# Latent attention: four rows of products a step, and every fourth division moved to VectorE

## What is computed

```
score  = sum over 8 index heads of wi * relu(qi . ki), causal      # choose 128 keys of a query
logits = q_lat . c_sel + bias[distance]                            # 16 heads, chosen keys only
p      = softmax(logits)
o_lat  = p . c_sel
o      = o_lat through w_uv per head;  out = o @ w_o
```

## Time and profile before

| what | value |
|---|---|
| median of three runs | 1882.61 us (1882.45 to 1882.95) |
| the profiled execution | 1882.13 us |
| its span on the core | 1880.9 us |
| PE busy | 1864.3 us, 99% of the span |
| DVE busy | 977.3 us, 52% |
| ACT busy | 674.5 us, 36% |
| POOL busy | 380.7 us, 20% |
| granted PE clock, mean | 0.999 |

### The profile page before, as it was taken

The page is one execution under the profiler, slowest core; times in us unless marked ns, Lnnn a source line. Parts: engine busy times, 40 slices in busy tenths (PEclk is TensorE's granted clock), DMA queues, the critical chain, the costliest instruction groups (busy, mean ns, idle before and its releaser), DMA issues.

```text
span 1880.9 us, 21858 instructions
## 1 busy us (share of the span) xinstructions
PE 1864.3 (99%) x8900; PEld 1503.8 (80%) x8900; DVE 977.3 (52%) x1318; ACT 674.5 (36%) x912; POOL 380.7 (20%) x339
## 2 busy tenths in 40 slices
PE   9999999999999999999999999999999999999998
PEld 8888888888877568888888879778787878888887
DVE  7885543343459864543433447666446454443432
ACT  6743222222234762321212334555323332322213
POOL 2004210010336783210101131111001311110103
PEclk9999999999999999999999999999999999999999
DMA  4322323323333103233232222222232322223221
GB/s 159 112 90 90 112 90 102 100 90 100 97 96 106 53 2 112 90 99 103 90 105 97 76 91 90 68 68 68 84 113 83 108 87 96 90 97 105 90 95 62
DMA packets 167171, 172.36 MB, mean 92 GB/s; under 512 B 7480, under 2 KB 164288, under 8 KB 167072
## 3 DMA queue, kind: packets, MB, share of 16 engines
q1 hardware_dynamic: 164576, 163.76, 27.1%
q0 software_dynamic: 2496, 7.21, 1.2%
HBM read 168.69 MB, written 2.14 MB: 91 GB/s over the span
## 4 chain that ended last, share of the span: by engine, by line
PE 89%; DVE 6%; ACT 3%; issue 2%; DMA 0%; POOL 0%; SPq 0%; DVEq 0%; ACTq 0%
PE bank L775 27%; PE bank L777 27%; PE bank L776 27%; DVE wlo L1699 1%; PE bank L800 1%; DVE XC L1801 1%; PE bank L994 1%; PE bank L1096 1%; PE bank L1113 1%; PE bank L973 1%; ACT whi L1217 1%; ACT pt L1437 1%; PE bank L922 0%; PE bank L1108 0%; PE bank L1162 0%
## 5 line engine op out<-in xcount | busy, mean ns | idle before, releaser
L775 PE MATMUL bank<-Ahi,whi 128*128 128x512 f32 (+2 forms) x1416 | 552.9, 390 | 2.5 <-DVE wlo L1699 0.9
L776 PE MATMUL bank<-Alo,whi 128*128 128x512 f32 (+2 forms) x1416 | 547.8, 387 | 0.0
L777 PE MATMUL bank<-Ahi,wlo 128*128 128x512 f32 (+2 forms) x1416 | 547.7, 387 | 0.0
L1699 DVE TENSOR_TENSOR wlo<-stage,whi 128x2048 fp32r<-128x2048 f32 (+2 forms) x146 | 333.1, 2281 | 381.5 <-ACT whi L1217 381.4
L1217 ACT ACTIVATE whi<-stage 128x2048 fp32r<-128x2048 f32 (+2 forms) x152 | 287.2, 1889 | 443.3 <-PE bank L777 443.3
L775 PEld LDWEIGHTS bank<-Ahi,whi 128*128 128x128 f32 (+1 forms) x1416 | 265.3, 187 | 65.6 <-issue 8.2
L777 PEld LDWEIGHTS bank<-Ahi,wlo 128*128 128x128 f32 (+1 forms) x1416 | 265.3, 187 | 55.1
L776 PEld LDWEIGHTS bank<-Alo,whi 128*128 128x128 f32 (+1 forms) x1416 | 265.4, 187 | 54.8 <-issue 1.2
L775 PE MATMUL bank<-Hhi,whi 128*128 128x512 f32 x688 | 267.7, 389 | 0.0
L777 PE MATMUL bank<-Hhi,wlo 128*128 128x512 f32 x688 | 267.6, 389 | 0.0
L776 PE MATMUL bank<-Hlo,whi 128*128 128x512 f32 x688 | 267.6, 389 | 0.0
(11 more groups left out here) (349 smaller groups left out, 2151.7 us busy)
## 6 DMA issues: line engine op xcount, KB each, us to landing
stage<-in_mlp_w_up SPq DMA_DIRECT2D x32, 1024.0 KB, 5.4
stage<-in_mlp_w_down SPq DMA_DIRECT2D x32, 1024.0 KB, 5.0
stage<-in_w_in SPq DMA_DIRECT2D x22, 1024.0 KB, 4.9
stage<-in_w_ffn_in SPq DMA_DIRECT2D x22, 1024.0 KB, 4.9
stage<-in_w_ffn_out SPq DMA_DIRECT2D x8, 1024.0 KB, 5.1
stage<-in_rec_w_in SPq DMA_DIRECT2D x7, 1024.0 KB, 5.1
stage<-in_att_w_in SPq DMA_DIRECT2D x6, 1024.0 KB, 5.4
stage<-in_rec_w_out SPq DMA_DIRECT2D x4, 1024.0 KB, 4.7
```

Source lines behind the costliest of these rows:

```text
L775: e.matmul(ps, hi, rh, start=first, stop=False)
L776: e.matmul(ps, hi, rl, start=False, stop=False)
L777: return e.matmul(ps, lo, rh, start=False, stop=last)
L1699: e.tensor_tensor(lo_of(u)[:, 0:nk, 0:n], stage[s][:, 0:nk, 0:n], f32(hi_of(u)[:, 0:nk, 0:n]), ALU.subtract).then_inc(s_lo[s], 1)
```

## The change

One step now takes four tiles. PE at step t: four key products, four penalties, for t < 4 both values products of block t, transposes of the four tiles of step t-1, then two gathers of the four tiles of step t-2. The ring is listed in that order: s, s, s, s, (val, val), t, t, t, t. The buffers `pT` grow from four places to eight, partly in a new tile `pTx`. DVE divides tiles 3, 7, 11, ... (`scale_p`, with the semaphore `s_pd`), POOL the other three of four. On DVE a step is soften and over_sum of four tiles, the division, then copies of values, `out_lo` and search rounds at the end; on ACT the copies of transposed tiles are set between the second and the third exponent and after the fourth. The end of the loop is written out: transposes of tiles 60 and 61, gathers, half an out product, then tiles 62 and 63. The number of products, exponents, copies and search rounds is as before.

```diff
--- before.py
+++ after.py
@@ -304,13 +304,13 @@
         if m == 3:
             ring.add(("uk", 0), ("uk", 1))
     ring.add(*[("K", c) for c in range(8)])
-    for t in range(34):
-        if t < 32:
-            ring.add(("s", 2 * t), ("s", 2 * t + 1))
-        if t < 8:
-            ring.add(("val", t // 2, t % 2))
-        if t >= 2:
-            ring.add(("t", 2 * t - 4), *([("wo", 0)] if t == 33 else []), ("t", 2 * t - 3))
+    for t in range(17):
+        if t < 16:
+            ring.add(*[("s", 4 * t + x) for x in range(4)])
+        if t < 4:
+            ring.add(("val", t, 0), ("val", t, 1))
+        if t >= 1:
+            ring.add(("t", 4 * t - 4), ("t", 4 * t - 3), *([("wo", 0)] if t == 16 else []), ("t", 4 * t - 2), ("t", 4 * t - 1))
     ring.add(*[("wo", m) for m in range(1, 8)])
     for m in range(4):
         u_end["wo", m] = ("wo", 2 * m + 1)
@@ -394,7 +394,7 @@
     s_pen, s_found = [sem(f"s_pen{j}") for j in range(4)], sem("s_found")
     s_sco = [sem(f"s_sco{j}") for j in range(4)]
     s_rel, s_relp, s_relw = sem("s_rel"), sem("s_relp"), sem("s_relw")
-    s_exp, s_rec, s_p, s_pv = (sem(n) for n in ("s_exp", "s_rec", "s_p", "s_pv"))
+    s_exp, s_rec, s_p, s_pd, s_pv = (sem(n) for n in ("s_exp", "s_rec", "s_p", "s_pd", "s_pv"))
     s_osh, s_osl = sem("s_osh"), sem("s_osl")
     s_tsa, s_tsp = sem("s_tsa"), sem("s_tsp")
     s_wd, s_wp, s_ic, s_cm = sem("s_wd"), sem("s_wp"), sem("s_ic"), sem("s_cm")
@@ -440,6 +440,7 @@
     pt = [pool("pt", kb, [128, S]) for kb in (80, 82, 94, 96)] + [at("pt", o_stage + (8 + 2 * i) * KB, [128, S]) for i in range(4)]
     pt0 = [pool("pt0", 2 * i + 1.5, [128, 128]) for i in range(8)]
     pT = [pool("pT", 98 + 2 * i, [128, 4, 128]) for i in range(4)]
+    pTx = pool("pTx", 64, [128, 8, S])
     cT = pool("cT", 80, [128, S])
     cvar = pool("cvar", 82, [128, S])
     ukT = pool("ukT", 102, [128, 8, 128])
@@ -518,6 +519,24 @@
 
         return tiles[i][0] == 3 and i % 2 == 1
 
+    def scaled_by_dve(i):
+        return i % 4 == 3
+    def pT_of(i):
+        j, b = tiles[i][0], i % 8
+        if j < 2:
+            return pT[b // 2][:, 2 * (b % 2):2 * (b % 2) + j + 1, :]
+        if b < 4:
+            return pT[b][:, 0:j + 1, :]
+        return pTx[:, 4 * (b % 2):4 * (b % 2) + j + 1, (b - 4) // 2 * 128:(b - 4) // 2 * 128 + 128]
+    def pT_read(i):
+        return 2 * i - 38 if 32 <= i < 36 else i - 7
     def p_of(i):
 
         j = tiles[i][0]
@@ -693,6 +712,8 @@
         lo(54)
         penalty(2)
         for i, (j, h) in enumerate(tiles):
+            if scaled_by_dve(i):
+                continue
             e.wait_ge(s_rec, i + 1)
             p = p_of(i)
             e.tensor_scalar(p, p, stat[:, i % 8, 2:3], None, ALU.mult).then_inc(s_p, 1)
@@ -959,11 +980,12 @@
                      start=True, stop=True).then_inc(*ring.put(("val", j, i)))
 
         def logits(t):
-            j = tiles[2 * t][0]
+            j = tiles[4 * t][0]
             nk = (j + 1) * 128
-            if t % 8 == 0:
+            if t % 4 == 0:
                 e.wait_ge(s_pen[j], 1)
-            for i in (2 * t, 2 * t + 1):
+            for i in range(4 * t, 4 * t + 4):
                 h = tiles[i][1]
                 p0 = (h % 2) * 64
                 ps = begin(("s", i))
@@ -971,12 +993,15 @@
                     e.wait_ge(*ring.free(("K", h // 2)))
                     e.wait_ge(*ring.free(("q", h // 2)))
                 e.matmul(ps[:, 0:nk], QT[p0:p0 + 64, h // 2, j * 128:(j + 1) * 128], KT[p0:p0 + 64, h // 2, 0:nk], start=True, stop=False)
-            for i in (2 * t, 2 * t + 1):
+            for i in range(4 * t, 4 * t + 4):
                 e.matmul(ring.bank(("s", i))[:, 0:nk], identb[:, :], pen[:, wk_off[j]:wk_off[j] + nk], start=False, stop=True).then_inc(*ring.put(("s", i)))
 
         def turn_p(i):
             j, h = tiles[i]
-            e.wait_ge(s_p, i + 1)
+            if scaled_by_dve(i):
+                e.wait_ge(s_pd, i // 4 + 1)
+            else:
+                e.wait_ge(s_p, i // 4 * 3 + i % 4 + 1)
             transposes(("t", i), [p_of(i)[:, k * 128:(k + 1) * 128] for k in range(j + 1)])
 
         def gather(t):
@@ -992,7 +1017,7 @@
             for k in range(j + 1):
                 for x in range(2):
                     i = e.matmul(banks[6 + g % 2][64 * x:64 * x + 64, c * 128:(c + 1) * 128], VT[:, k, (h + x) * 64:(h + x + 1) * 64],
-                                 pT[(2 * t + x) % 4][:, k, :], start=(k == 0), stop=(k == j))
+                                 pT_of(2 * t + x)[:, k, :], start=(k == 0), stop=(k == j))
                     if k == j:
                         i.then_inc(s_pv, 1)
 
@@ -1008,25 +1033,30 @@
             if half:
                 i.then_inc(*ring.put(("wo", m)))
 
-        for t in range(32 + 3):
-            if t < 32:
-                logits(t)
-            if t < 8:
-                values_of(t // 2, t % 2)
-            if 2 <= t < 34:
-                turn_p(2 * t - 4)
-                if t == 33:
-                    gather(30)
-                    e.wait_ge(s_osl, 7)
-                    out_half(0, 0)
-                turn_p(2 * t - 3)
-            if t == 34:
-                out_half(1, 0)
-                gather(31)
-                out_half(2, 0)
-                out_half(3, 0)
-            elif 3 <= t < 33:
-                gather(t - 3)
+        for t in range(16):
+            logits(t)
+            if t < 4:
+                values_of(t, 0)
+                values_of(t, 1)
+            if t >= 1:
+                for i in range(4 * t - 4, 4 * t):
+                    turn_p(i)
+            if t >= 2:
+                gather(2 * t - 4)
+                gather(2 * t - 3)
+        turn_p(60)
+        turn_p(61)
+        gather(28)
+        gather(29)
+        e.wait_ge(s_osl, 7)
+        out_half(0, 0)
+        turn_p(62)
+        turn_p(63)
+        out_half(1, 0)
+        gather(30)
+        gather(31)
+        out_half(2, 0)
+        out_half(3, 0)
         e.wait_ge(s_osl, 8)
         for m in range(4):
             out_half(m, 1)
@@ -1439,29 +1469,29 @@
         def copy_pT(i):
             j, h = tiles[i]
             e.wait_ge(*ring.full(("t", i)))
-            if i > 3:
-                e.wait_ge(s_pv, i - 3)
-            e.activation(pT[i % 4][:, 0:j + 1, :].rearrange("p a c -> p (a c)"), ring.bank(("t", i))[:, 0:(j + 1) * 128], ACT.Copy).then_inc(*ring.take(("t", i)))
+            if i > 7:
+                e.wait_ge(s_pv, pT_read(i))
+            e.activation(pT_of(i), ring.bank(("t", i))[:, 0:(j + 1) * 128].rearrange("p (a c) -> p a c", c=128), ACT.Copy).then_inc(*ring.take(("t", i)))
 
         def copy_out_hi(g):
             j, c0_ = g // 2, g % 2 * 4
             e.wait_ge(s_pv, 8 * g + 8)
             e.activation(OSh[:, c0_:c0_ + 4, j * 128:(j + 1) * 128], banks[6 + g % 2][:, :].rearrange("p (c q) -> p c q", c=4), ACT.Copy).then_inc(s_osh, 1)
 
-        for t in range(32 + 3):
+        for t in range(18):
             if t == 0:
                 copy_values(0)
-            if t < 32:
-                exponent(2 * t)
-                exponent(2 * t + 1)
-            if t < 8 and t % 2 == 0 and t:
-                copy_values(t // 2)
-            if 2 <= t < 34:
-                copy_pT(2 * t - 4)
-                if not by_dve(2 * t - 3):
-                    copy_pT(2 * t - 3)
-            if t >= 3 and (t - 3) % 4 == 3:
-                copy_out_hi((t - 3) // 4)
+            for x in (0, 2):
+                if t < 16:
+                    exponent(4 * t + x)
+                    exponent(4 * t + x + 1)
+                for i in (4 * t - 4 + x, 4 * t - 3 + x):
+                    if 1 <= t < 17 and not by_dve(i):
+                        copy_pT(i)
+            if 0 < t < 4:
+                copy_values(t)
+            if t >= 3 and t % 2 == 1:
+                copy_out_hi((t - 3) // 2)
         for what, m in product_order(8):
             if what == "w" and m:
                 hi(u_of["wo", m] + 1)
@@ -2005,8 +2035,8 @@
 
         def copy_pT(i):
             e.wait_ge(*ring.full(("t", i)))
-            e.wait_ge(s_pv, i - 3)
-            e.tensor_copy(pT[i % 4][:, :, :].rearrange("p a c -> p (a c)"), ring.bank(("t", i))[:, :]).then_inc(*ring.take(("t", i)))
+            e.wait_ge(s_pv, pT_read(i))
+            e.tensor_copy(pT_of(i), ring.bank(("t", i))[:, :].rearrange("p (a c) -> p a c", c=128)).then_inc(*ring.take(("t", i)))
 
         def out_lo(g):
             j, c0_ = g // 2, g % 2 * 4
@@ -2021,27 +2051,34 @@
             e.wait_ge(*ring.full(label))
             e.tensor_copy(VT[:, j, 512:1024], ring.bank(label)[:, :]).then_inc(*ring.take(label))
 
-        for t in range(32 + 3):
-            if t < 32:
-                soften(2 * t)
-                if t:
-                    over_sum(2 * t - 1)
-                soften(2 * t + 1)
-                over_sum(2 * t)
-            if t == 32:
-                over_sum(63)
-            if 2 <= t < 34 and by_dve(2 * t - 3):
```

(30 more changed lines are left out.)

## The result

| | before | changed |
|---|---|---|
| median | 1882.83 us (6 runs) | 1895.70 us (6 runs, 1894.32 to 1898.20) |
| the profiled execution, its span | 1882.13, 1880.9 | 1898.20, 1897.0 |
| PE / DVE / ACT / POOL busy | 1864.3 / 977.3 / 674.5 / 380.7 | 1866.4 / 987.1 / 674.1 / 362.9 |

The ratio is 1.007, interval 1.006 to 1.008: slower by 12.9 us, where 8.9 was forecast. The changed kernel's six executions differ with their mean granted clock: 1894.3 us at 0.999, 1894.5 at 0.998, 1895.6 and 1895.8 at 0.995, 1898.0 at 0.994 and 1898.2 at 0.995. The profiled one is the longest of them.

What follows compares the result with a forecast made beforehand. It took DVE to bound block 1 and block 2's first half, PE block 3. Block 0 +4.2, block 1 +4.05, block 2 +3.0, block 3 -2.3 gave +8.9 us: median 1891.5, own range 1887 to 1895, outer 1884 to 1896.

Steps and rivals of the forecast that it cites:

- DVE's step: Blocks 1 and 2: DVE waits in order behind exponents, copies and division; +4.05 us and +3.0 us.
- the loop through the copies of values: Block 0: a key product needs the bank DVE empties at its step's end; 5.2 us a step, +4.2 us.
- the sum: Block 1: step of 3.57 us (first 3.36), plus search rounds of 1.38 and two `out_lo`; 20.8 us against 16.74.
- The tail: Block 3 to the third half product: PE's saved starts shorten 36.3 to 34.0 us, -2.3 us.
- The likeliest case: Whole kernel: the forecast itself, +8.9 us to 1891.5 us, chance 0.70, own range 1887 to 1895.
- Its two terms: Own range: division at 512 keys 0.32 to 0.68 gives -1 to +3; block 0 loop 5.0 to 5.6, -1 to +1.
- The outer one: Whole kernel: range 1884 to 1896 us, holding the forecast and (a), leaving out (b) and (c).
- PE idle in the stage some 15 us more: Attention stage: sign of being right, in gaps before the third transposed tile and the second key product.
- the one row at 666.52: Block 2, kernel before: a DVE scaling of 0.41 us during POOL's division; taken to show DVE did not wait.
- (c): Whole stage: DVE is no bound, PE's saved starts count everywhere; -7.7 us, 1875; chance 0.11.
- (b): DVE's step: exponents and waits overlap as before, costing only the old 2.34 and division's 0.46; 1883; chance 0.12.
- (a): Blocks 1 and 2: DVE's division waits for POOL's in flight, 0.31 and 0.51 us; +2.8 us, 1894.3; chance 0.07.

Runs made afterwards that it cites:

- the clock held: Changed kernel, in which PE repeats products and transposes, with the same results, in places where it waited: 1893.89 us.
- e7: Changed kernel without its ten search rounds inside the attention steps (block 3 then chooses fewer keys): 1883.78 us.
- e3: Changed kernel, but POOL does all 64 divisions again: 1891.03 us.
- e2: Changed kernel, but ACT does all four exponents of a step first, then the four copies of transposed tiles: 1891.95 us.
- e4: Changed kernel, but in steps 0 to 3 ACT copies values right behind the second exponent, DVE right behind the fourth soften: 1892.14 us.
- e9: Changed kernel; POOL divides in blocks 0 to 2; block 0 exponents first, values copied early; blocks 1 and 2 search round behind the fourth soften: 1879.30 us.
- e5: Changed kernel; blocks 0 to 2 exponents first, POOL divides; values copied early; one search round at the end of each of steps 1 to 10: 1883.99 us.
- e10: Kernel before, two tiles a step, but DVE divides every fourth tile right behind its reciprocal: 1883.78 us.
- e11: e9, but DVE divides every fourth tile in all blocks, as in the changed kernel: 1880.65 us.

## Why the prediction was right and wrong

**Right: the sign and the mechanism of the slowdown, as far as the forecast had it.** DVE's step sets blocks 1 and 2, the loop through the copies of values sets block 0, and PE gains only in block 3. With the clock held, the steps of block 1 are 5.39, 5.07, 5.67 and 5.07 us where the sum has 5.34, 4.95, 5.55 and 4.95. e7 shows DVE as the bound, e3 the division, e2 in part the wait behind the copies, e4 the loop through the copies of values. The tail was forecast at 34.0 and is 34.3.

**Wrong: the size, 8.9 us against 12.9.** The likeliest case's own range, 1887 to 1895, does not hold 1895.7. (Its two terms, added to 1891.5, give 1889.5 to 1895.5 and not the range stated.) The outer one does by 0.3, and that is luck, since neither range had room for the clock. Two steps failed; together they are 3.9 of the 4.0 us.

The first was missing altogether: PE's clock. My part on what bounds the kernel read a granted clock of 1.00 and kept it, although I wrote, as a sign to look for, "PE idle in the stage some 15 us more". That sign was met: gaps of 1.1 to 2.8 us, and PE's busy time from 618 to 728 us fell from 107.5 to 93.3. I did not ask what that idleness does to PE itself. Holding the clock took 1.8 us off the median and 4.3 off the stretches of the profiled execution.

The second is the price of DVE's division beside POOL's, and with it two smaller prices: with the clock held, the stretches sum to 103.2 instead of 101.1, 2.1 us more. I took a division of 384 keys at 0.33 between starts from the output's scaling; three of the four took about 0.75 busy, and the two of these with work right behind them 0.66 to the next start: 0.66 of the 1.05 us that block 2 is over. Of 256 keys I took 0.27, and they took 0.31 once and 0.39 three times: all of the 0.4 us of block 1. The other price in block 2 is that of two search rounds in a row, 2.91 us and not 2.76, twice. Block 0 and the tail are 0.3 us over each.

That DVE's division would lose nothing beside POOL's I drew from the one row at 666.52. That instruction is the penalty, with a bf16 output, and it takes the same 0.41 us in the changed kernel, where POOL is idle (687.02). So it lost nothing, but the f32 division does not behave like it, as the last section shows.

**The rivals.** (c), faster, had no support once DVE's step was 5 us. (b), the waits overlap as before, did not hold for the order of the change, but e9 comes near it: there a search round fills the wait. (a), DVE waits for POOL's division in flight, had a sign of its own, a division of 384 keys far above 0.40 busy, and the mean was 0.665. Its wait was not there: the division starts 0.20 us behind the start of its reciprocal, as forecast. But it is stretched, by 0.12 us in block 1 and 0.33 in block 2, where (a) had 0.31 and 0.51. So (a) is half right, and its 1894.3 is near the held median of 1893.89 by chance.

**The rule weighed.** The lock for a whole instruction that the forecast quotes from the Trainium skill (SBUF — State Buffer, section "SBUF: two separate sides") did not show for DVE: none of its divisions waited for the end of POOL's. What I drew from that, no cost at all, was wrong.

## What to carry to other kernels

When a change lengthens the unit of work of an ordered pipeline, write out one step of each engine's list and sum the waits in it: what one engine may do while it waits for another is decided by what stands next in its list, and a filler such as the search round belongs into that wait, not behind it. Halving PE's group starts brings little on an engine that then waits for banks. And if a forecast adds gaps to PE's stream, it must say what the clock will do.

## What the runs showed that I had not expected

PE's clock fell behind gaps of 1.6 us with work on either side, stayed at 1.2 GHz over most of four microseconds of full work and came back to 2.4 GHz while that work went on. The same gap had a fall behind it in one trace (e9) and none in another (e5). The changed kernel's times spread over 3.9 us, against 1.1 for the kernel before and 0.7 with the clock held, which fits falls that come in some executions more often than in others.

DVE's division beside POOL's, of 384 keys both, in the changed kernel:
```profile
670.19 0.42 DVE L2057 TENSOR_SCALAR pt<-pt,stat 128x384 f32<-128x384 f32 x1
...
678.11 0.75 DVE L2057 TENSOR_SCALAR pt<-pt,stat 128x384 f32<-128x384 f32 x1
```
POOL's, beside them:
```profile
670.37 1.36 POOL L719 TENSOR_SCALAR pt<-pt,stat 128x384 f32<-128x384 f32 x1
...
678.06 1.24 POOL L719 TENSOR_SCALAR pt<-pt,stat 128x384 f32<-128x384 f32 x1
```
The first began in the last 0.18 us of one of POOL's, before its next: it took 0.42 us, and POOL's next one 1.36 instead of 1.24. The second began 0.05 us behind the start of POOL's and took 0.75, without waiting for POOL's end at 679.30. The other runs have further starting points. Here are the same division in e10, in e11 and in e2:
```profile
660.47 0.42 DVE L2009 TENSOR_SCALAR pt<-pt,stat 128x384 f32<-128x384 f32 x1
...
660.49 0.42 DVE L2060 TENSOR_SCALAR pt<-pt,stat 128x384 f32<-128x384 f32 x1
...
663.80 0.68 DVE L2056 TENSOR_SCALAR pt<-pt,stat 128x384 f32<-128x384 f32 x1
```
In e10 POOL does nothing beside any of the four, and each takes 0.42 us: that is its price alone. In e11 three start together with POOL's to the hundredth: DVE's take 0.42, and POOL's 1.45, 1.45 and, with the penalty on DVE beside it as well, 1.71. In e2 all four start 0.77 to 0.79 us behind the start of one of POOL's and take 0.67 or 0.68, where a wait to POOL's end and then 0.42 would make 0.89. So in these runs DVE's division of 384 keys keeps its 0.42 us when it starts with POOL's or just ahead of it, and then POOL's is the longer one; begun 0.05 or 0.8 us behind POOL's, it is stretched by 0.33 or 0.26 us, less than a full wait. No run varies this start alone, so what lies between these points stays open.
